# A hybrid attention and expert layer: attention units, gate copies and cache loads placed anew in the list of steps

## The reference, cut to what matters

```python
s = jnp.einsum('bqhd,bkhd->bhqk', q, k).astype(F32) * (D_F ** -0.5)
s = s + (jnp.swapaxes(fq, 1, 2)[:, :, :, None] - jnp.swapaxes(fk, 1, 2)[:, :, None, :])
...
p = jax.nn.softmax(s, axis=-1).astype(v.dtype)
return jnp.einsum('bhqk,bkhd->bqhd', p, v)
...
merged = (gates[..., 0, :] * (o_r @ w_br_ret)
          + gates[..., 1, :] * (o_f @ w_br_fox)
          + gates[..., 2, :] * (o_m @ w_br_mem))
```

## Time and profile before

| | |
|---|---|
| three runs | 712.43, 712.62, 710.84 us (median 712.43) |
| the profiled execution | 710.56 us, span 708.8 us, mean granted clock 0.979 |
| busy | TensorE 660.3 us (93%), VectorE 346.2 us (49%), ScalarE 259.0 us (37%), Pool 120.1 us (17%) |
| DMA | 175.61 MB, mean 248 GB/s; over 420 GB/s in most of the last 200 us |

### The profile page before, as it was taken

The page is one execution under the profiler, slowest core; times in us unless marked ns, Lnnn a source line. Parts: engine busy times, 40 slices in busy tenths (PEclk is TensorE's granted clock), DMA queues, the critical chain, the costliest instruction groups (busy, mean ns, idle before and its releaser), DMA issues.

```text
span 708.8 us, 9451 instructions
## 1 busy us (share of the span) xinstructions
PE 660.3 (93%) x3512; PEld 438.0 (62%) x3512; DVE 346.2 (49%) x733; ACT 259.0 (37%) x501; POOL 120.1 (17%) x129
## 2 busy tenths in 40 slices
PE   5999999989999899998899999889998999898895
PEld 4878888778887666667777878643443443343331
DVE  4748449964465454544446752764233433233211
ACT  5673433253334445445944322542211211121100
POOL 0019326660002010000000010004003102101100
PEclk9999999999999899999999999899999999999998
DMA  8956333452115333213767379468999999999980
GB/s 317 391 221 227 130 118 115 138 205 108 61 61 203 131 120 112 75 53 119 267 239 282 124 287 421 196 246 339 420 423 421 420 421 421 419 421 420 422 374 23
DMA packets 34048, 175.61 MB, mean 248 GB/s; under 512 B 4256, under 2 KB 4400, under 8 KB 20816
## 3 DMA queue, kind: packets, MB, share of 16 engines
q1 hardware_dynamic: 30896, 163.29, 59.1%
q0 software_dynamic: 3104, 11.68, 4.7%
HBM read 167.99 MB, written 7.48 MB: 248 GB/s over the span
## 4 chain that ended last, share of the span: by engine, by line
PE 74%; issue 9%; DMA 8%; DVE 4%; ACT 3%; SPq 1%; POOL 1%; DVEq 0%; ACTq 0%; POOLq 0%
PE banks L1530 13%; PE banks L1866 13%; PE banks L1531 13%; PE banks L1532 13%; DMA wgu<-in_wexp 8%; PE banks L1890 6%; PE banks L1854 2%; PE banks L1718 1%; PE banks L1803 1%; PE banks L1691 1%; ACT z L923 1%; PE banks L1732 1%; SPq L749 1%; PE banks L1604 1%; PE banks L1901 1%
## 5 line engine op out<-in xcount | busy, mean ns | idle before, releaser
L1133 DVE TENSOR_TENSOR w_lo<-raw,w_hi 128x1024 fp32r<-128x1024 f32 (+1 forms) x81 | 128.5, 1598 | 85.1 <-ACT w_hi L896 84.9
L1866 PE MATMUL banks<-wgu,xs 128*64 128x512 f32 x512 | 122.3, 608 | 6.7 <-DMA wgu<-in_wexp 6.7
L1530 PE MATMUL banks<-w_hi,hT_hi 128*128 128x512 f32 x312 | 126.1, 404 | 0.7 <-DVE w_lo L1133 0.6
L1531 PE MATMUL banks<-w_lo,hT_hi 128*128 128x512 f32 x312 | 123.1, 395 | 0.0
L1532 PE MATMUL banks<-w_hi,hT_lo 128*128 128x512 f32 x312 | 122.9, 394 | 0.0
L896 ACT ACTIVATE w_hi<-raw 128x1024 fp32r<-128x1024 f32 x79 | 83.4, 1056 | 88.8 <-PE banks L1532 84.8
L1866 PEld LDWEIGHTS banks<-wgu,xs 128*64 128x64 f32 x512 | 42.2, 140 | 83.7 <-issue 68.7
L1530 PEld LDWEIGHTS banks<-w_hi,hT_hi 128*128 128x128 f32 x312 | 59.8, 192 | 14.6 <-DVE w_lo L1133 1.5
L1532 PEld LDWEIGHTS banks<-w_hi,hT_lo 128*128 128x128 f32 x312 | 59.5, 191 | 12.9
L1531 PEld LDWEIGHTS banks<-w_lo,hT_hi 128*128 128x128 f32 x312 | 59.8, 192 | 11.7
L1890 PE MATMUL banks<-wdn,act_T 128*64 128x512 f32 x256 | 58.5, 598 | 1.1
(11 more groups left out here) (336 smaller groups left out, 985.2 us busy)
## 6 DMA issues: line engine op xcount, KB each, us to landing
wgu<-in_wexp SPq DMA_DIRECT2D x64, 1024.0 KB, 21.7
raw<-in_wstream SPq DMA_DIRECT2D x79, 512.0 KB, 3.9
wdn<-in_wexp SPq DMA_DIRECT2D x32, 1024.0 KB, 21.6
foxc<-in_foxc POOLq DMA_DIRECT2D x8, 512.0 KB, 4.2
memv<-in_memc SPq DMA_DIRECT2D x8, 512.0 KB, 4.8
memk<-in_memc SPq DMA_DIRECT2D x8, 512.0 KB, 5.5
xT<-in_xT SPq DMA_DIRECT2D x1, 1536.0 KB, 11.4
xtok<-in_xtok SPq DMA_DIRECT2D x1, 1536.0 KB, 7.9
```

What stands on the lines that cost most here:

```text
L1133: dve.tensor_tensor(w_lo[:, i % PART_SLOTS, cols], raw[:, i % RAW_SLOTS, cols], w_hi[:, i % PART_SLOTS, cols].bitcast(F32), ALU.subtract). ...
L1530: mm(out, xh, wh, start=start, stop=False, skip_group_check=True)
L1531: mm(out, xh, wl, start=False, stop=False, skip_group_check=True)
L1866: ins = mm(ps[64 * e2:64 * e2 + 64, 2 + a % 2, :], xs[:, (a // 2) % 2, k, c0:c0 + CAP], wgu[e % EXP_SLOTS][:, 512 * k:512 * k + 512], star ...
```

## The change

In the loop that weaves units and granules, `unit_p` stands at the front of a step, for the unit two steps back, instead of at the end for the unit one step back; the values of row units come one step later, and so does `unit_o`. Parts 0 to 3 are spread over steps 8, 12, 16 and 20 (before: 3 to 6); parts 4 to 7 come in steps 29, 30, 31 and 31 (before: 28 to 31). The copies of a gate chunk are held back until the next `unit_p` has been listed. The first two granules among the turns come one turn earlier each. At the end of the list `unit_p`, `unit_v` and the sigmoids around granules 60 to 62 are placed anew. On the Pool queue the wait for the stored state now stands behind the first two cache loads, and the four buffers are used in the order 3, 2, 0, 1.

```diff
     for i in range(20):
         s.append(("turn", i))
-        if i in (5, 12, 19):
+        if i in (4, 11, 19):
             gate()
...
-    def gate():
+    def gate(evacs=s):
         g = next(gates)
         granule(g)
         if g + 1 in FIRST:
-            s.append(("evac", chunk_at[g]))
+            evacs.append(("evac", chunk_at[g]))
...
-    oT_parts = {3 + j: j for j in range(4)} | {last_fox + 3 + j: 4 + j for j in range(4)}
+    oT_parts = {8 + 4 * j: [j] for j in range(4)} | {last_fox + 4: [4], last_fox + 5: [5], last_fox + 6: [6, 7]}
...
     for i in range(early):
+        if i >= 2:
+            pieces.append(("unit_p", i - 2))
         if i >= 1:
             pieces.append(("unit_w", i - 1))
         pieces.append(("unit_s", i))
-        for j in (i - 3,):
-            if 0 <= j:
-                pieces.append(("unit_v" if units[j][0] in ("foxp", "memp") else "unit_o", j))
-        for j in (i - 2,):
-            if 0 <= j and units[j][0] in ("foxs", "mems"):
-                pieces.append(("unit_v", j))
-        if i >= 1:
-            pieces.append(("unit_p", i - 1))
-        if i in oT_parts:
-            pieces.append(("parts", oT_parts[i]))
+        if i >= 4 and units[i - 4][0] in ("foxs", "mems"):
+            pieces.append(("unit_o", i - 4))
+        if i >= 3:
+            pieces.append(("unit_v", i - 3))
+        pieces += [("parts", j) for j in oT_parts.get(i, [])]
...
         s.append(piece)
         scores += piece[0] == "unit_s"
+        if piece[0] == "unit_p":
+            s += evacs
+            evacs = []
         if piece[0] == "unit_s":
...
-                gate()
+                gate(evacs)
+    s += evacs
...
-    s += [("mem_caches",), ("unit_w", n - 1), ("unit_v", n - 3), ("gates", 0), ("gates", 1)]
+    s += [("mem_caches",), ("unit_p", n - 2), ("unit_w", n - 1), ("unit_v", n - 3), ("gates", 0)]
     granule(r)
-    s += [("gates", 2), ("unit_p", n - 1), ("unit_v", n - 2)]
+    s += [("unit_p", n - 1), ("unit_v", n - 2), ("gates", 1)]
     granule(r + 1)
-    s += [("gates", 3), ("gates", 4), ("gates", 5)]
     merge(r + 1)
-    s += [("unit_s", n)]
+    s += [("gates", 2), ("gates", 3), ("gates", 4), ("gates", 5), ("unit_v", n - 1), ("unit_s", n)]
     granule(r + 2)
-    s += [("unit_v", n - 1), ("unit_w", n), ("unit_s", n + 1)]
+    s += [("unit_w", n), ("unit_s", n + 1)]
...
+        def fox_slot(b):
+
+            return (3, 2, 0, 1)[b % 4]
...
-                    pool.wait_ge(s_state_out, 32)
                     pool.wait_ge(s_out, 16 * 4)
...
-                    for b in range(4):
-                        store(foxc[b][:, :], io["foxc"][b], foxc_in[b])
+                    for b in range(2):
+                        store(foxc[fox_slot(b)][:, :], io["foxc"][b], foxc_in[fox_slot(b)])
                     pool.memset(qb_f[:, :, :, :], 0.0)
                     chain(pool.memset(qb_m[:, :, :, :], 0.0))
+                    pool.wait_ge(s_state_out, 32)
+                    for b in range(2, 4):
+                        store(foxc[fox_slot(b)][:, :], io["foxc"][b], foxc_in[fox_slot(b)])
```

More of the change, by code:

```diff
@@ L151, in schedule @@
     last_fox = max(j for j, u in enumerate(units) if u[0] == "foxs")
-    oT_parts = {3 + j: j for j in range(4)} | {last_fox + 3 + j: 4 + j for j in range(4)}
+    oT_parts = {8 + 4 * j: [j] for j in range(4)} | {last_fox + 4: [4], last_fox + 5: [5], last_fox + 6: [6, 7]}
+    assert last_fox + 6 < early
     for i in range(early):
+        if i >= 2:
+            pieces.append(("unit_p", i - 2))
         if i >= 1:
@@ L1479, in _ @@
                     pool.wait_ge(u_v, i + 1)
-                    store(foxc[b % 4][:, :], io["foxc"][b], foxc_in[b % 4])
+                    store(foxc[fox_slot(b)][:, :], io["foxc"][b], foxc_in[fox_slot(b)])
                 elif kind == "merge" and i >= C_BR + 4:
@@ L1696, in _ @@
                         pe.wait_ge(qb_ready, a + 1)
-                        pe.wait_ge(foxc_in[a % 4], 16 * (a // 4 + 1))
+                        pe.wait_ge(foxc_in[fox_slot(a)], 16 * (a // 4 + 1))
                         mm(bank[:, 0:P], headsel, nf_c[:, a, :], start=True, stop=False, **kw)
@@ L1700, in _ @@
                         for hp in range(4):
-                            mm(bank[32 * hp:32 * hp + 32, 0:P], qb_f[:, a % 2, hp, :], foxc[a % 4][:, hp * P:(hp + 1) * P], start=False, stop=True, **kw)
+                            mm(bank[32 * hp:32 * hp + 32, 0:P], qb_f[:, a % 2, hp, :], foxc[fox_slot(a)][:, hp * P:(hp + 1) * P], start=False, stop=True, **kw)
                         for hp in range(4):
@@ L1738, in _ @@
                         for hp in range(4):
-                            mm(bank[32 * hp:32 * hp + 32, 0:P], pr[:, 32 * hp:32 * hp + 32], foxc[a % 4][:, 512 + hp * P:512 + (hp + 1) * P], start=True, stop=False, **kw)
+                            mm(bank[32 * hp:32 * hp + 32, 0:P], pr[:, 32 * hp:32 * hp + 32], foxc[fox_slot(a)][:, 512 + hp * P:512 + (hp + 1) * P], start=True, stop=False, **kw)
                         for hp in range(4):
```

## The result

| | before | changed |
|---|---|---|
| runs with the first profile | 712.52 us, median of 4 (710.84 to 712.92) | 700.02 us, median of 4 (697.64 to 701.56) |
| profiled execution | 710.56 us, span 708.8 | 699.08 us, span 697.3 |

The ratio is 0.9835, with a 95% interval of 0.9807 to 0.9863: the change makes the kernel faster by 12.5 us. The forecast was 703.4 us in a range of 700.0 to 708.5. Against the profiled execution the forecast was 701.5, and 699.08 was measured.

A forecast was written before the change was run, and what follows sets the result against it. Expert weights were taken to set the pace from 465 us, TensorE with its waits and slow clock the attention stretch. 2.2 + 6.1 + 0.8 - 0.8 + 0.75 + 0 = 9.0 us off 712.43 gave 703.4, range 700.0 to 708.5.

The forecast's parts named there:

- What was left alone: Unit loop: scores, weightings, turnings, weight granules and splits behind the turns keep their sequence, so moving unit_p changes nothing there.
- Turns: Granules one turn earlier: 1.7 of wait and 1.6 of slow clock go, 1.1 of new wait comes; gain 2.2 us.
- Gate copies and parts: Attention stretch: gate copies behind the probability copy gain 6.1 us; moved parts gain 0.8 and lose 0.8.
- The lost waits of the new parts: Parts 0 and 3 cost 0.7 us in step 8 and 0.1 in step 20; a wait of 1.06 stays later.
- Row units: Values matmuls one step later fill part of the 1.30 us wait before 320.17; gain 0.75 us, bound 0.
- The end of the list: Granule 60 waits about 1.4 us, the 1.85 wait goes, granule 64 is unmoved; gain 0, bounds -1.5 and +1.
- The path that the forecast added up: ScalarE's chain through unit 32's exponential and merge 16 puts granule 64 at 25.1 us behind granule 59, as before.
- Cache loads: Pool queue: two of four loads issued before the state's store has landed change nothing; 0, at worst 1 us once.
- The mis-sized term: Slow clock stretches: those near 157 and 242 us should go, 1.6 us each; the one near 232 was kept.
- Rival 1: The clock falls elsewhere, in the new block of turns or after 242.2: 705.0 or 706.6 us; chance 0.25.
- slow stretches as many as before: Sign of being wrong: the changed profile shows no fewer stretches of slow clock than the old one.
- Rivals 2 to 4: ScalarE's queue at the list's end, 707 (0.1); expert weights swallow the gain, 712.4 (0.06); row units slow the clock, 716 (0.04).

The follow-up runs named there:

- u_evacs: Changed kernel with each gate copy directly behind its granule again, parts left as changed; 701.87 us.
- b_evacs: Kernel before with only the gate copies held back behind the next unit_p; 707.92 us.
- u_parts: Changed kernel with parts 0 to 3 back in steps 3 to 6; 699.17 us.
- better: Changed kernel with parts 6 and 7 behind the copies of chunk 14 and the first sigmoid, last three sigmoids behind granule 67; 700.42 us.
- u_tail: Changed kernel with the old order of sigmoids, unit 31's values and granules 60 to 62, parts 6 and 7 as changed; 699.8 us.
- after_again: The changed kernel run once more without any edit; 698.57 us.
- u_rows: Changed kernel with values and turning back of the row units one step earlier again; 700.75 us.
- after: The changed kernel as first run and profiled; median 700.02 us, profiled execution 699.08 us.

## Why the prediction was right

**What was left alone.** That scores, weightings and turnings keep their order is a matter of the two lists, and the marks agree: two falls and the waits at gate copies, parts, row units and the end of the list make up 9.75 of the 9.84 us from U to G64.

**Turns, forecast 2.2, measured 2.06 in the profiles.** The parts: wait in front of the granule 0.85 (0.7), new wait 0.89 (1.1), fall gone. The sum is right, but its certain part is 0.37, where the forecast had 0.6; the rest was the fall, which the old order of the turns has in two of four profiles and the new one in none of ten.

**Gate copies and parts.** The reading of the queues held, piece by piece, in u_evacs, b_evacs and u_parts. The wait of 2.13 and those of 0.96 and 1.47 are gone. What the forecast put down to the copies alone at chunk 11 belongs to copies and parts together. The lost waits of the new parts were over-priced: 0.31 for 0.7 in step 8, none for 0.1 in step 20, 0.77 for 1.06 at the later parts.

**Row units, 0.75.** Undone alone 0.66; the rest of the old 1.30 is now a wait of 0.74 for the `o_rows` copy, of which the forecast gave 0.1 to that place.

**The end of the list, 0.** The wait of 1.39 before granule 60 (1.4), and none of 1.85. G64 stood 0.29 nearer behind granule 59's last matmul: 25.13 after 25.42. The profile names oT_lo for the 1.39. But granule 60 waits for parts 0 and 1 alone, done long before (the four slabs are complete only for granule 61), and for its bank, of which the gate copies of chunk 14 are the last readers; they stand behind parts 6 and 7, and the first of the three (0.68 each) ends near 330.1, where granule 60 starts at 330.21:

```profile
328.56 0.94 ACT L1019 ACTIVATE oT_hi<-oT 128x384 fp32r<-128x384 f32 x2
329.40 1.82 ACT L929 ACTIVATE z<-banks,small 128x512 f32<-128x512 f32 x3
```

In better, with the parts moved away, the wait is put down to the gate copy. The path that the forecast added up (17.7 + 6.8 + 0.6 = 25.1 through unit 32's exponential and merge 16) is not the one that bounds granule 64: it shows no wait in the changed profile, and better, whose exponential comes earlier, doesn't bring it forward. The chain and TensorE's own work end within about 0.3 us of each other (merge 16 starts at 351.56, granule 64 at 352.46), so the right number is in part luck. The forecast of 0 also hides that the new order of the sigmoids is worth 1.3 (u_tail), against which stands the new wait of 1.39.

**Cache loads, 0.** Measured 0.

**The mis-sized term** is the clock. The forecast counted two falls as gone (3.2) and kept the third at 232; it took 1.6 each, and a fall costs 1.7 (22.79 - 21.10). In the changed profile all three are missing, 5.1. That is 1.9 of the 2.4 by which the profiled execution beat the forecast. The over-priced parts (0.8) and the end of the list (0.3) would make it more; the turns, the row units and what was lost behind G64 took some of that back. Of the three, the one near 242 goes with a wait that the change removes: it or one like it, starting between 237 and 242, stood behind the long wait at chunk 11 in all four profiles of kernels that have that wait, in u_evacs behind one of 0.76, and in none of the nine other profiles. This is what 14 profiles have in common; no run tests it by itself. The one near 230 comes and goes with the same work in front of it. What decides it is not shown.

**The rivals.** Rival 1, that the clock falls elsewhere, came in part, and where it costs little. In the turns it was the wrong way round: the new block of turns 5 to 11 with its wait kept the full clock in all nine profiles that have it. By the rule of the Trainium skill (TensorE: Matmul & The Clock Gate, Part 4: PE-mode transpose) that transposes don't count as activity as matmuls do, it would have been at risk; no profile here bears that out. The fall near 242 didn't move to another place before G64 either. But over the whole execution the changed profile has as much slow clock as the one before (0.979 both), most of it in the stage of the experts. The forecast named "slow stretches as many as before" as a sign of being wrong; it stays away only up to G64. after_again has neither the fall near 535 nor the one near 593 and takes 237.9 us from the first expert matmul to the end, 1.3 less; yet this stage took 237.9 to 241.0 in the 14 profiles, the 241.0 in u_rows with one fall of 6.8 in it, so not all of that spread is clock. Rivals 2 to 4 are out: the gain before G64 arrived at the end but for 0.7 us. Too small was the forecast's 2.1 us for what a measurement can tell: executions of the kernel before differed by 9.

## What to carry to other kernels

When one list of steps feeds in-order engines, compare the order of each kind of step before pricing a reordering: here the part that the edit seemed to be about changed nothing, and the side steps (copies and splits set between a producer and the instruction that a third engine waits for) gave nearly all of what isn't clock. Price an instruction on such a queue by who stands behind it and by the next independent work of the waiting engine, and look for chains of two: gate copies cost 0.8 us, with the parts behind them 2.1 to 2.5. Where executions differ by falls of the clock, lengths between marks on the bounding engine repeat within 0.1 us and tell parts of 0.4 us apart that medians of four runs can't.

## What the runs showed of the hardware

The kernel before took anything from 705.37 to 714.4 us. Its two executions with a mean clock of 0.993 took 705.66 and 706.34; most others, at 0.967 to 0.985, took 708.7 to 714.4. The changed kernel took 697.64 at 0.989 and 696.95 at 0.991. So between executions with nearly full clock 8.0 to 9.4 of the 12.5 us remain; 9.84 + 2.06 - 5.1 = 6.8 of it lie between T and G64 in the profiles. At a mean clock of 0.979 to 0.985 the kernel before took 708.73 to 714.4 and the changed one 698.33 to 701.56, so the mean clock alone doesn't tell the time: 3.4 us of slow clock cost 1.7 where TensorE is the bound, and two falls of 6.8 in the stage of the experts some 1.3 together (after against after_again, one pair).

A slow stretch can be twice as long: 6.8 us behind the wait of 2.53 in b_evacs, at a mean granted clock of 0.51, that is 1.2 GHz nearly throughout.

```profile
237.70:244.50 6.80, 5.93 (x15) 4.47 (x16) 3.84 (x11) 2.61 (x7) 0.00 (x0) 0.51 0.08 34
```

A change of ScalarE's table cost 1.28 us, and the next activation started 0.02 us behind it (450.36 and 451.66). The Trainium skill (ScalarE: Activation LUTs, What ACT_TABLE_LOAD costs) adds a drain of 1.38 us to each; no such time stands behind this load.
